# Other places for attention, merge and search among the fetch units of a product-key block, and other shares of their sums for VectorE

## The reference, cut to what matters

```python
h   = rmsnorm(x, norm_mix)
b_g, c_g, x_in, q_lat, kv_lat, kr_raw, gate_c, gate_a = in_projection(h, w_in)
attn = prompt_attention(...)      # causal; sample_attention over a paged cache for the short sequences
x = x + (sigmoid(gate_c) * ((b_g * conv_y) @ w_conv_out)
         + sigmoid(gate_a) * (attn @ w_attn_out)) @ w_mix_out          # branch_merge
# peer_block, h = rmsnorm(x, norm_ffn), per token:
q = (h @ w_peer_q).reshape(t, 8, 2, 128)
s = jnp.einsum('thcd,chnd->thcn', q, sub_keys)
s1, i1 = lax.top_k(s[:, :, 0], 16);  s2, i2 = lax.top_k(s[:, :, 1], 16)
best, sel = lax.top_k(all 256 sums s1 + s2, 16)                        # 16 experts for each of 8 heads
g = jax.nn.softmax(best)
a = gelu(jnp.einsum('thkd,td->thk', expert_u[eidx], h))
x = x + jnp.einsum('thk,thkd->td', g * a, expert_v[eidx])
```

## The kernel before, in words

| chunk | stage | before: units (VectorE) | after: units (VectorE) |
|---|---|---|---|
| 1 | attention | 0-84: 85 (38) | 0-46: 47 (19) |
| 1 | merge, gates and products | 85-135: 51 (22) | 47-92: 46 (34) |
| 1 | mixing and norm | 136-159: 24 (12) | 93-115: 23 (18) |
| 1 | search | 160-226: 67 (8) | 116-220: 105 (12) |
| 1 | end | 227-255: 29 (0) | 221-255: 35 (18) |
| 2 | attention | 256-414: 159 (71) | 256-362: 107 (49) |
| 2 | merge, gates and products | 415-479: 65 (33) | 363-423: 61 (40) |
| 2 | mixing and norm | 480-510: 31 (15) | 424-452: 29 (21) |
| 2 | search | 511-597: 87 (10) | 453-590: 138 (16) |
| 2 | end | 598-639: 42 (0) | 591-639: 49 (25) |
| 3 | paged attention | 640-877: 238 (111) | 640-877: 238 (111) |
| 3 | merge, mixing, norm | 878-932: 55 (23) | 878-932: 55 (35) |
| 3 | search | 933-980: 48 (6) | 933-980: 48 (6) |
| 3 | end | 981-1023: 43 (0) | 981-1023: 43 (22) |

## Time and profile before

### The profile page before, as it was taken

One profiled execution on the slowest core, in us unless ns is written; L12 is line 12 of the kernel. 1 busy time (PEld: TensorE's weight loads), 2 busy tenths in 40 slices (PEclk: granted clock), 3 DMA queues, 4 the chain that ended last, 5 costly groups with the idle time before them and its releaser, 6 DMA issues.

```text
span 4031.5 us, 36425 instructions
## 1 busy us (share of the span) xinstructions
PE 3336.6 (83%) x10788; PEld 1820.2 (45%) x10788; DVE 2542.3 (63%) x5428; ACT 1439.1 (36%) x4284; POOL 1153.7 (29%) x1316
## 2 busy tenths in 40 slices
PE   7987979947789998777778989877888878887887
PEld 4653337824445544333444445433444434465431
DVE  2104531477855699677766677994777677745874
ACT  1012221127822333356662233333444444422343
POOL 0000000033322343433333334442333233323442
PEclk9998968978899999887889999988988889887999
DMA  2011124449999998999999999999999898999999
GB/s 107 16 58 32 38 63 123 129 153 407 409 361 357 403 387 330 366 405 402 413 374 420 426 406 403 373 357 380 358 361 373 332 370 334 389 383 416 426 420 387
DMA packets 230961, 1274.64 MB, mean 316 GB/s; under 512 B 45356, under 2 KB 61292, under 8 KB 95157
## 3 DMA queue, kind: packets, MB, share of 16 engines
q0 software_dynamic: 152064, 1107.36, 67.6%
q1 hardware_dynamic: 76980, 160.67, 11.3%
q10 hardware_dynamic: 1728, 4.39, 0.3%
HBM read 1256.76 MB, written 15.56 MB: 316 GB/s over the span
## 4 chain that ended last, share of the span: by engine, by line
PE 35%; DMA 24%; DVE 14%; issue 6%; ACT 4%; POOL 1%; SPq 1%; POOLq 0%; ACTq 0%; DVEq 0%
DMA tl_uv<-in_uv,tl_idx 21%; PE tl_y L1002 14%; PE tl_f L1236 7%; DVE tl_uv L1567 3%; PE tl_f L1247 3%; PE tl_f L1262 2%; DVE tl_acc L1554 2%; DMA X<-in_krope 2%; PE tl_f L1062 1%; DVE tl_picked L1651 1%; DMA w_tail<-in_w_merge 1%; PE tl_f L1172 1%; PE tl_f L1195 1%; PE tl_f L1114 1%; POOL tl_uv L926 1%
## 5 line engine op out<-in xcount | busy, mean ns | idle before, releaser
L1567 DVE CUSTOM_DVE_ANT_0 tl_uv<-tl_uv,tl_h 128x1024 f32<-128x1024 f32 x1056 | 1272.3, 1218 | 766.0 <-DMA tl_uv<-in_uv,tl_idx 734.5
L1002 PE MATMUL tl_y<-tl_uv,tl_diag 128*128 128x512 f32 (+1 forms) x2828 | 1454.9, 657 | 247.5 <-ACT tl_diag L1283 243.1
L926 POOL DMA_INDIRECT tl_uv<-in_uv,tl_idx x1056 | 1039.9, 985 | 1927.8 <-PE tl_y L1002 1466.3
L1002 PEld LDWEIGHTS tl_y<-tl_uv,tl_diag 128*128 128x128 f32 (+1 forms) x2828 | 548.5, 205 | 983.6 <-issue 564.4
L1311 ACT ACTIVATE tl_ge<-tl_a 128x1 f32<-128x1 f32 x1056 | 209.2, 198 | 1174.9 <-DVE tl_a L1567 1151.0
L1554 DVE SCALAR_TENSOR_TENSOR tl_acc<-tl_uv,tl_w,tl_acc 128x1024 f32<-128x1024 f32 x341 | 436.9, 1281 | 62.6 <-ACT tl_w L1295 62.3
L1295 ACT ACTIVATE tl_w<-tl_ge,tl_weight 128x1 f32<-128x1 f32 x1024 | 301.5, 294 | 33.2
L1283 ACT ACTIVATE tl_diag<-K,tl_w 128x128 f32<-128x128 f32 (+1 forms) x707 | 281.3, 398 | 48.8 <-PE tl_y L1002 26.4
L1236 PE MATMUL tl_f<-H,w_tail 128*128 128x384 f32 (+2 forms) x1024 | 268.6, 419 | 31.4 <-DMA w_tail<-in_w_merge 30.2
L1262 PE MATMUL tl_f<-H,w_tail 128*128 128x384 f32 (+2 forms) x1024 | 265.5, 414 | 8.4 <-DVE H L1748 8.4
L938 POOL TENSOR_TENSOR tl_cand<-tl_tv 128x48 f32<-128x48 f32 (+5 forms) x128 | 27.7, 247 | 778.0 <-DVE tl_ti L1599 778.0
(11 more groups left out here) (216 smaller groups left out, 3250.2 us busy)
## 6 DMA issues: line engine op xcount, KB each, us to landing
w_tail<-in_w_merge SPq DMA_DIRECT2D x96, 512.0 KB
w_tail<-in_w_peer SPq DMA_DIRECT2D x64, 576.0 KB
tl_uv<-in_uv,tl_idx POOLq DMA_INDIRECT x1056
w_tail<-in_w_mix SPq DMA_DIRECT2D x32, 512.0 KB
X<-in_cache SPq DMA_DIRECT2D x64, 128.0 KB
w_conv<-in_w_conv SPq DMA_DIRECT2D x4, 1536.0 KB, 10.0
X<-in_x SPq DMA_DIRECT2D x8, 536.0 KB, 7.2
o_y<-tl_acc ACTq DMA_DIRECT2D x8, 512.0 KB
```

Source lines behind the costliest of these rows:

```text
L926: pool.indirect_dma_start(UV[:, u % RING, :], None, d["uv"], bass.IndirectOffsetOnAxis(ap=which, axis=0)).then_inc(landed[u % RING], 16)
L1002: mm = pe.matmul(Y[0:m, half * 512:(half + 1) * 512], DG[:, (pe_count[u] - 1) % DIAGS, 0:m], UV[:, u % RING, D + half * 512:D + (half + 1) ...
L1567: dve.tensor_tensor_reduce(UV[:, u % RING, 0:D], UV[:, u % RING, 0:D], HP[:], 1.0, 0.0, ALU.mult, ALU.add, A[:, t % 2, i:i + 1]).then_inc( ...
```

## The change

It replaces the numbers in `TICK` for chunks 0 to 2 (chunk 0 has no units beside it) and the rule `by_dve`. In attention the numbers of the items fall (in chunk 1 from 12 to 7, in chunk 2 from 18 to 13) and those of its five last steps from 8 to 5, the 16 search steps rise from 16 to 27 and the last four from 8 to 14. `by_dve` gives VectorE three units in four from the merge's start to the search (before: one in two), one in eight in the search as before, and one in two after the search's end (before: none). The row of `TICK` for chunk 3 stays. Two lines are added, so lines from L805 on have numbers higher by 2.

```diff
--- before.py
+++ after.py
@@ -780,8 +780,8 @@
 
         DEC = 9 * NSEQ + 3
         PRE = [len(x) + 5 for x in items] + [DEC]
-        TICK = [[6 + 2 * PARTS[c][1]] * len(items[c]) + [8] * 5
-                + [8, 8, 4, 4] * KD + [12] + [8] * KD + [16] + [16] * HC + [8] * 4 + [0] for c in range(NCH - 1)]
+        TICK = [[2 * PARTS[c][1] + 1] * len(items[c]) + [5] * 5
+                + [8, 8, 4, 4] * KD + [12] + [8] * KD + [16] + [27] * HC + [14] * 4 + [0] for c in range(NCH - 1)]
         TICK.append([10, 10, 12, 10, 12, 14, 12, 22, 12] * NSEQ + [20, 14, 12]
                     + [6, 6, 3, 3] * KD + [16] + [6] * KD + [16] + [12] * HC + [12] * 4 + [0])
         passed = [[0] + list(itertools.accumulate(x)) for x in TICK]
@@ -802,9 +802,11 @@
             c = chunk_of(u // PICK) + 1
             if c == NCH or u % PICK < 8:
                 return False
-            if u < due(c, RANK, 0):
-                return u % 2 == 1
-            return u < due(c, END, 0) and u % 8 == 7
+            if due(c, MERGE, 0) <= u < due(c, RANK, 0):
+                return u % 4 != 0
+            if due(c, RANK, 0) <= u < due(c, END, 0):
+                return u % 8 == 7
+            return u % 2 == 1
 
         pe_count = list(itertools.accumulate(0 if by_dve(u) else 1 for u in range(UNITS)))
         dve_units = list(itertools.accumulate(1 if by_dve(u) else 0 for u in range(UNITS)))
```

## The result

| | median | range | runs |
|---|---|---|---|
| before | 4047.91 us | 4028.32 to 4067.33 | 4 |
| after | 4136.84 us | 4133.13 to 4146.61 | 4 |

The ratio is 1.0224, with a 95% interval of 1.0171 to 1.0277. The change makes the kernel slower, by about 90 us between the medians. The forecast was 4024 us, in a range of 3985 to 4073: it has the wrong sign, and the measured time lies outside the range.

The account below looks back on a forecast made before the run. The prediction took DMA as the bound, with other engines near their limits where it is short of full. Chunks 1, 2 and 3 gave -5 - 14 - 2 = -21 us: 4013 us, or 4024 as a median, range 3985 to 4073.

Parts of the forecast that it names:

- DMA sets it: 297: Chunk 1's search: with 38 more units, DMA transfers are the fullest resource and set 297 us, +80.
- 375: Chunk 2's search: with 51 more units, DMA work of 374 us sets the stage, taken as 375, +113.
- the buffers last over its bursts of search work: Chunk 1's search: six or seven units a step, VectorE's share falling from 0.93 to 0.86, keep DMA supplied.
- rival 3: Searches: VectorE's bursts still open the DMA, shares stay 0.94 and 0.95; 316 and 393 us, total +16; chance 0.20.
- Rival 2: Searches stay at their old rates, 370 and 383 GB/s: 325 and 402 us, total +34, 4079 us; chance 0.08.
- 147 / 0.92 = 160: Chunk 1's attention: ScalarE's 147 us of work at a 0.92 share sets 160 us, -70.
- DMA sets it; I take 304: Chunk 2's attention: with 52 fewer units, DMA's 300 us still sets the stage, taken as 304, -127.
- Rival 1: Chunk 1's attention: TensorE waits for exp at every item; 210 us, total +29, 4074 us; chance 0.15.
- turning point of 181: Length of chunk 1's attention, in us, from which Rival 1 turns the forecast's sign; measurably slower from 201.
- DMA sets it: Chunk 1's merge: DMA's 157 us, above TensorE's 135, sets the stage, taken as 160 us, -22.
- 197 - 10: Chunk 2's merge: DMA was full, so going from 65 to 61 units gives 187 us, -10.
- another engine is near its limit: Stages where DMA is short of full, including chunk ends at 0.88 and 0.94: another engine is nearly saturated.

Follow-up runs that it names:

- after_ring9_fine: Changed kernel with nine gather buffers instead of eight and VectorE's search work cut in five pieces in chunks 0 to 2: 4051.35 us, ratio 1.0017.

## Why the prediction was wrong

**The searches: the step that failed first.** "DMA sets it: 297" and "375" rested on the sentence that with six or seven units to a step "the buffers last over its bursts of search work". They didn't. More units between the pieces don't make a piece shorter, and the DMA can only work ahead by the buffers that are free when the piece begins. The rows to see it in were there: ScalarE's longest wait for a product was 14.2 us already before, against eight buffers of 2.45 us, some of which are held between product and sum. A share of engine work over a stage's length can't tell this. The DMA shares stayed near 0.94 and 0.95 (0.92 and 0.94 now), as rival 3 had said, but the lengths are even above its 316 and 393. The kernel before has the same pieces: in chunk 1's search ScalarE waits seven times for 6 to 14 us on a product, and by slices of 1 us the DMA falls short of full by 17 us there, where it is 31 now. Why a piece empties the DMA more than before is not shown by any run. An added unit cost (326 - 217) / 38 = 2.87 us in chunk 1 and (405 - 262) / 51 = 2.80 in chunk 2. The forecast's +80 and +113 are 2.1 and 2.2 us a unit, since they also counted on the DMA's gaps to fill. This is +29 and +30 us.

**Rival 2 had the number and not the mechanism.** It gave 325 and 402 us and a total of 4079. If memory had limited the searches to 370 and 383 GB/s, neither a ninth buffer nor another order on VectorE could have helped. Both did, and together brought 401 and 417 GB/s. By the page "DMA: Bandwidth & Descriptors" of the Trainium skill, section "Where 436 GB/s comes from", memory would bind at about 358 GB/s, a figure that the section works out as the 716 GB/s of a memory stack over its two cores. This kernel runs on one core, and its search at 417 GB/s for 370 us (chunk 2, after_ring9_fine) lies above that figure.

**The attentions: the second step that failed.** "147 / 0.92 = 160" took for ScalarE a share that TensorE and VectorE reach in other stages. (The prediction calls 0.92 to 0.93 the best of the rows, but TensorE has 1.00 in chunk 1's mixing; no row has a stage that ScalarE limits.) ScalarE reached 140 / 176 = 0.80. For chunk 2, "DMA sets it; I take 304" missed that the DMA would no longer be full: 0.94, and 323 us. Rival 1 named the place and a part of the mechanism: the transposes' waits for exp rose from 17.5 to 31.3 us. Larger, and in no part of the prediction, is VectorE's wait for weights, which rose from 1.7 to 48.4 us. Rival 1 also put the length at 210, where 176 was measured, which is below its own turning point of 181. Six of an item's seven us are ScalarE's own work. Which wait of the circle sets the rest, and what order would remove it, stays open: both other pairs of lags were worse, and buffer and cuts left the length as it was.

**The sum of it.** A unit taken out of attention gave back (230 - 176) / 38 = 1.42 us in chunk 1 and (431 - 323) / 52 = 2.08 in chunk 2; in the search it cost 2.8 to 2.9. The prediction had -70 and -127 against +80 and +113, where -54 and -108 against +109 and +143 were measured. The step behind both was to let the busy time of the fullest resource set the length of a stage. In the attention of before the transfers were the longest chain, and the other engines' waits ran beside them and cost nothing. With fewer transfers these waits show.

**The merges.** Chunk 1's length is right: 162 for 160. It is the rule that brings it: 162 and 165 us with the rule alone, 173 with the places alone, where 182 was before. But the reason given, "DMA sets it", isn't borne out, so the number is partly luck. The DMA share is 0.93, and TensorE's is 0.94 instead of the 0.85 forecast, with 152 us of work for 135. Chunk 2's is wrong, 205 for "197 - 10". Its beginning shows a part of it. First the kernel before, then after, in windows of 10 us around TensorE's wait for the merge's first weights:

```profile
2123.00:2133.00 10.00, 6.09 (x14) 3.57 (x15) 4.10 (x7) 0.00 (x0) 0.00 (x0) 0.65 1.02 424
2133.00:2143.00 10.00, 10.00 (x29) 5.32 (x28) 6.15 (x9) 4.51 (x17) 3.26 (x3) 1.00 0.98 389
```

```profile
2035.00:2045.00 10.00, 10.00 (x43) 7.17 (x43) 2.29 (x3) 8.00 (x19) 2.60 (x2) 0.67 0.16 34
...
2065.00:2075.00 10.00, 8.32 (x17) 4.71 (x18) 0.00 (x0) 0.00 (x0) 0.00 (x0) 0.63 0.55 229
2075.00:2085.00 10.00, 10.00 (x30) 5.51 (x29) 7.26 (x10) 3.70 (x15) 3.97 (x4) 1.00 0.80 283
```

The wait for weights is nearly the same, 14.0 us for 12.9, but attention now ends with a nearly empty DMA (0.16), and 20 us into the merge come 20 us at 256 GB/s. Against the 423 GB/s of before that is 8 us; a second such stretch from 2145 to 2175 us, at 327 GB/s, is 7 more (by the DMA shares the two are 6.5 and 2.6 us). The places bring the loss: this merge takes 211 us with the places alone and 196 with the rule alone. What in the order makes the two stretches is not settled, since no run changed the units there alone.

**Ends and chunk 3.** The ends came out as worked out (104 and 133 for 101 and 133). The prediction's sentence that in each of the stages short of full another engine is near its limit doesn't hold for them: before, no engine was busy for more than 0.76 of an end. Its sum didn't use it. Chunk 3 was to lose 2 us and has 11 more. 7 of these are its paged attention, whose units and rule the change leaves as they are: it took 736 us in the profile before and 740 to 748 in the profiles with eight buffers since, of old places and new. I take it for the difference between executions, which no run shows. Its merge got nothing from the rule: 192 us with the mixing, as with the rule alone (192) and with the places alone (193), against 186.

## What to carry to other kernels

When work is moved between stages, price it twice: by what the giving stage refunds and by what the receiving stage charges. The price of a full DMA holds only where the transfers stay full on both sides, and a stage that is full now may not be so with less work behind it. Beside the busy shares of an engine, read the longest stretch in which it serves no buffer, and compare it with the time that the buffers in flight can bridge. Test the parts of a change alone: here a rule worth about 10 to 20 us was hidden under a loss of 105.

## What the runs showed that was not expected

- A ninth buffer of 1.05 MB is worth 58 us on the new places (4137 to 4079) and 32 on the old (4031 to 3998); by the ratios to the kernel before in each group it is 53 and 27. At the old places it does little for chunk 1's search (2 us), where VectorE is busy for 0.93, and gives 13 us in the paged attention.
- Cutting VectorE's piece gains 20 us on the new places, but nothing on the old ones, and chunk 3's search, which was full, gets 5 to 7 us longer with it.
- Two units less of lag cost 100 us, and the two attentions alone are 105 longer (234 and 370 us for 176 and 323). Two more cost 41 us, of which the attentions have 17 (181 and 335).
- In chunk 1's attention VectorE is part of the circle of waits while it is busy for only 0.59 of the stage.
